# First norm's row factors moved behind the first matrix products of a fp32-split kernel, with nine low parts on GpSimd

## The reference, cut to what matters

```
xn = rmsnorm(x, norm1_g)                 # x * rsqrt(mean(x*x) + 1e-6) * g, per token
u  = xn @ w_in                           # 1024 x 5632
q_sb, k_sb, v_sb, f_raw, i_hg, q_hg, g_hg, gate_sb, gate_hg = split(u)
o_sb = stick_breaking_attention(q_sb, k_sb, v_sb)      # 8 heads of 64
o_hg = rmsnorm(hgrn2(silu(q_hg), 1-f, i_hg, log f)) * silu(g_hg)   # 4 heads of 128
h  = x + (sigmoid(gate_sb+b)*(o_sb @ w_o_sb) + sigmoid(gate_hg+b)*(o_hg @ w_o_hg)) @ w_out
```

## Time and profile before

| | |
|---|---|
| median of 3 runs | 1062.19 us (1062.15 to 1062.34) |
| the profiled execution's own time | 1062.51 us |
| its span in the trace | 1060.6 us |
| PE busy | 1049.5 us, 99% |
| DVE busy | 714.8 us, 67% |
| ACT busy | 596.8 us, 56% |
| POOL busy | 57.3 us, 5% |

### The profile page before, as it was taken

One profiled execution on the slowest core, in us unless ns is written; L12 is line 12 of the kernel. 1 busy time (PEld: TensorE's weight loads), 2 busy tenths in 40 slices (PEclk: granted clock), 3 DMA queues, 4 the chain that ended last, 5 costly groups with the idle time before them and its releaser, 6 DMA issues.

```text
span 1060.6 us, 16168 instructions
## 1 busy us (share of the span) xinstructions
PE 1049.5 (99%) x6582; PEld 926.2 (87%) x6582; DVE 714.8 (67%) x835; ACT 596.8 (56%) x754; POOL 57.3 (5%) x53
## 2 busy tenths in 40 slices
PE   9999999999999999999999999999999999999998
PEld 8897999888888889888888888899998888888888
DVE  6547786675656567966666666677888676666564
ACT  7558554454444356865754444476776564444464
POOL 0000001110000030002005000010000200000010
PEclk9999999999999999999999999999999999999999
DMA  8735444646564656345465565555424455555651
GB/s 270 257 120 184 134 159 126 213 137 220 173 221 161 200 162 207 127 128 201 159 198 200 186 210 190 168 173 185 160 81 154 134 185 198 173 199 174 211 171 41
DMA packets 131274, 184.32 MB, mean 174 GB/s; under 512 B 3200, under 2 KB 107904, under 8 KB 131200
## 3 DMA queue, kind: packets, MB, share of 16 engines
q1 hardware_dynamic: 130752, 182.68, 51.9%
q0 software_dynamic: 160, 0.52, 0.2%
q10 hardware_dynamic: 288, 0.07, 0.0%
HBM read 182.21 MB, written 1.05 MB: 173 GB/s over the span
## 4 chain that ended last, share of the span: by engine, by line
PE 90%; DVE 5%; ACT 3%; issue 2%; DMA 1%; SPq 0%; DVEq 0%; ACTq 0%
PE PS L375 88%; PE PS L383 2%; DVE WL L1730 1%; ACT WH L1129 1%; DMA RAW<-in_gla_w_in_dram 0%; DMA H<-in_x_dram 0%; DVE AR L1968 0%; DVE AR L2160 0%; ACT AR L1144 0%; DVE AR L2158 0%; DVE SC L2352 0%; ACT H L1439 0%; ACT X L1138 0%; DVE X L1742 0%; DVE AR L2152 0%
## 5 line engine op out<-in xcount | busy, mean ns | idle before, releaser
L1730 DVE TENSOR_TENSOR WL<-RAW,WH 128x2048 fp32r<-128x2048 f32 (+1 forms) x170 | 375.4, 2211 | 139.1 <-ACT WH L1129 138.6
L1129 ACT ACTIVATE WH<-RAW 128x2048 fp32r<-128x2048 f32 (+1 forms) x177 | 326.3, 1848 | 82.0 <-PE PS L375 77.6
L375 PE MATMUL PS<-WH,X 128*128 128x512 f32 (+1 forms) x1168 | 307.4, 346 | 0.6 <-issue 0.4
L375 PE MATMUL PS<-O,WH 128*128 128x512 f32 (+1 forms) x880 | 265.7, 363 | 0.2 <-DVE WL L1730 0.2
L375 PEld LDWEIGHTS PS<-WH,X 128*128 128x128 f32 x1168 | 204.6, 190 | 28.3 <-issue 2.1
L375 PE MATMUL PS<-X,WH 128*128 128x256 f32 (+1 forms) x864 | 218.2, 331 | 0.5 <-ACT X L1138 0.5
L375 PE MATMUL PS<-O,WL 128*128 128x256 f32 x744 | 203.3, 282 | 0.0
L375 PE MATMUL PS<-WL,X 128*128 128x512 f32 (+1 forms) x584 | 200.7, 344 | 0.0
L375 PEld LDWEIGHTS PS<-O,WH 128*128 128x128 f32 x880 | 156.1, 189 | 25.1 <-issue 0.7
L375 PE MATMUL PS<-X,WL 128*128 128x256 f32 x608 | 167.6, 282 | 0.0
L375 PEld LDWEIGHTS PS<-X,WH 128*128 128x128 f32 x864 | 145.1, 190 | 15.6 <-issue 0.9
(11 more groups left out here) (215 smaller groups left out, 764.0 us busy)
## 6 DMA issues: line engine op xcount, KB each, us to landing
RAW<-in_ffn_w_in_dram SPq DMA_DIRECT2D x44, 1024.0 KB, 5.1
RAW<-in_w_ff_dram SPq DMA_DIRECT2D x32, 1024.0 KB, 5.4
RAW<-in_ffn_w_out_dram SPq DMA_DIRECT2D x22, 1024.0 KB, 5.1
RAW<-in_w_in_dram SPq DMA_DIRECT2D x20, 1024.0 KB, 5.1
RAW<-in_gla_w_in_dram SPq DMA_DIRECT2D x12, 1024.0 KB, 5.3
RAW<-in_diff_w_in_dram SPq DMA_DIRECT2D x12, 1024.0 KB, 5.3
RAW<-in_ple_w_gate_dram SPq DMA_DIRECT2D x8, 1024.0 KB, 5.1
RAW<-in_w_out_dram SPq DMA_DIRECT2D x4, 1024.0 KB, 5.0
```

Source lines behind the costliest of these rows:

```text
L375: return e.matmul(o, l, r, start=start, stop=stop, skip_group_check=skip)
L1129: act(high, raw, ACT.Copy).then_inc(s["w_hi"], 1)
L1730: e.tensor_tensor(low, raw, high.bitcast(F32), ALU.subtract).then_inc(s["w_lo"], 1)
```

## The change

x is turned raw as it lands: first the blocks of x0, then of x1, and ACT and DVE split the turned blocks with the gain alone. DVE computes the row factors later (`first_norm`, after the low part of chunk 2), lays them out as RB by way of PE and ACT, and applies them where the products are read: a DVE `evac` multiplies the bank by RB for the 256-column forms (16 in all), ACT's `evac` of the long chunks (4, 5, 10 to 13) takes the factor as its scale. The gates' tanh stays on ACT, now in place in SBUF. The first chunk's first piece is loaded between x0 and x1, and the constants go ahead of chunk 4 where they went ahead of chunk 5. The low parts of chunks 6, 8, ... 22 of w_in move from DVE to POOL. Chunks 0 to 3 get banks 0, 1, 5, 6. The warm-up matmuls at the start are 8 and 3 where they were 24.

```diff
-POOL_LO = [AT["w_o_hg"] + 1, ...
+POOL_LO = [*(AT["w_in"] + n for n in range(6, 23, 2)), AT["w_o_hg"] + 1, ...
@@ tensor_program
-    for _ in range(WARM):                      # WARM = 24
-        mm(PS[:, 3, 0:128], m.ar(0, 128), m.ar(0, 128), True, True)
+    warm(WARM[0])                              # WARM = 8, 3
     e.wait_ge(s["d_idn"], 16)
+    e.wait_ge(s["d_x0"], 16)
+    turn_x(0, range(7))
+    warm(WARM[1])
+    e.wait_ge(s["d_x1"], 16)
+    first_chunk()
...
-    for n in range(4):
+    for n in range(1, 4):
         win(n)
+    e.wait_ge(s["d_con"], 16)
+    spread_r("n1", 2)
     first(4)
-    e.wait_ge(s["win_ev"], 4)
+    e.wait_ge(*evacuated(3))
     scores(0)
@@ scalar_program
     hi(w0 + 2)
-    evac(0)
     hi(w0 + 3)
-    evac(1)
+    rstd_y("n1")
+    spread_copy(0, 2)
     hi(w0 + 4)
-    evac(2)
     hi(w0 + 5)
...
     hi(w0 + 6)
     softplus(0)
@@ vector_program
+    def evac(n):
+        j, i = n % 2, n - 14
+        e.wait_ge(s["rb"], 1)
+        e.wait_ge(s["gemm"], w0 + n + 1)
...
+        e.scalar_tensor_tensor(out=dst, in0=v3(PS[:, WIN_BANK[n], :], 2), scalar=0.125 if n < 2 else 1.0,
+                               in1=m.RB[:, :].unsqueeze(1).to_broadcast([128, 2, 256]), op0=ALU.mult,
+                               op1=ALU.mult).then_inc(s["win_c"], 1)
-    for n in range(2, 6):
-        lo(w0 + n)
+    lo(w0 + 2)
+    first_norm()
+    lo(w0 + 3)
+    spread_diag(0, rstd_r("n1"))
+    lo(w0 + 4)
+    for n in range(4):
+        evac(n)
+    lo(w0 + 5)
     bounds()
-    lo(w0 + 6)
     softplus(0)
     lo(w0 + 7)
-    lo(w0 + 8)
     masked(0)
     softplus(1)
+    evac(6)
@@ gpsimd_program
+    for c in range(AT["w_in"] + 6, AT["w_in"] + 23, 2):
+        lo(c)
@@ sync_program
+    e.dma_start(H[:, 0, :], x_rows[:, 0, :]).then_inc(s["d_x0"], 16)
+    piece(0, 0)
+    e.dma_start(H[:, 1, :], x_rows[:, 1, :]).then_inc(s["d_x1"], 16)
```

More of the change, by code:

```diff
@@ L543, in spread_r, with turn_x, warm, first_chunk @@
         e.wait_ge(s["rb_d"], i + 1)
[L544 removed]
+        mm(PS[:, bank, 0:256], m.con("none"), m.ar(13888 if i < 2 else 8192, 256), True, True).then_inc(s["rb_m"], 1)
+    def turn_x(tb, ks):
+        for k in ks:
+            i = tr(turn_src(m, "n1", k)[:, 128 * tb:128 * tb + 128], m.tok(m.H)[:, tb, 128 * k:128 * k + 128])
+            if tb == 1:
+                i.then_inc(s["tr"], 1)
+    def warm(n):
+        for _ in range(n):
+            mm(PS[:, 0, 0:128], m.ar(0, 128), m.ar(0, 128), True, True)
+    def first_chunk():
+        (wh, wl), (high, low) = m.weights(0), m.pair("X")
+        for k in range(8):
+            turn_x(1, ((0, 1, 2, 3), (4, 5), (6,))[k] if k < 3 else ())
+            if k == 3:
+                turn_x(0, (7,))
+                turn_x(1, (7,))
+            if k % 2 == 0:
+                e.wait_ge(s[hi_done(0, k // 2)[0]], hi_done(0, k // 2)[1])
+            e.wait_ge(s["tr_hi"], k + 1)
+            for fb in range(2):
+                mm(PS[:, 0, fb * 256:fb * 256 + 256], wh[:, k, fb * 128:fb * 128 + 128], high[:, k, :], k == 0 and fb == 0, False, True)
+            if k % 2 == 0:
+                e.wait_ge(s[lo_done(0, k // 2)[0]], lo_done(0, k // 2)[1])
+            for fb in range(2):
+                mm(PS[:, 0, fb * 256:fb * 256 + 256], wl[:, k, fb * 128:fb * 128 + 128], high[:, k, :], False, False, True)
+            e.wait_ge(s["tr_lo"], k + 1)
+            for fb in range(2):
+                i = mm(PS[:, 0, fb * 256:fb * 256 + 256], wh[:, k, fb * 128:fb * 128 + 128], low[:, k, :], False, k == 7, True)
+        i.then_inc(s["gemm"], 1)
     e.wait_ge(s["warm"], 1)
[L548 to L549 removed]
+    warm(WARM[0])
     e.wait_ge(s["d_idn"], 16)
+    e.wait_ge(s["d_x0"], 16)
[3 more added lines that the diff above has]
+    first_chunk()
     qT, kT, v = (m.ar(o, 1024) for o in (0, 1024, 2048))
@@ L1825, in vector_program @@
     e.memset(m.ar(0, 128), 0.0).then_inc(s["warm"], 1)
[L1826 to L1839, removed]
-    e.wait_ge(s["d_g1"], 16)
[L1841 to L1855, removed]
+    lo(0, 0)
+    e.wait_ge(s["d_g1"], 16)
+    for j in range(4):
+        if j:
+            lo(0, j)
+        turn_lo("n1", 2 * j, 2 * j + 1)
+    for j in range(4):
+        lo(1, j)
     kh, qh, lf, bb, vh, GS, fr, ng = (m.ar(6528 + 1024 * i, 1024) for i in range(8))
@@ L2022, in vector_program @@
     factors(4)
+    evac(17)
     level(2)
     spans(6)
-    lo(w0 + 20)
     level(3)
+    evac(18)
     factors(5)
@@ L2031, in vector_program @@
     level(4)
-    lo(w0 + 22)
+    evac(19)
+    evac(20)
     level(5)
@@ L2036, in vector_program @@
     lo(w0 + 23)
+    evac(21)
     lo(w0 + 24)
@@ L2574, in sync_program @@
             e.wait_ge(s[lo_done(c - NR)[0]], lo_done(c - NR)[1])
-        n = PIECES.get(c, 1)
-        for j in range(n):
-            k1, kn = k0 + j * nk // n, nk // n
-            src = io[name][k1 * 128:(k1 + kn) * 128, n0:n0 + nn].rearrange("(k p) n -> p k n", p=128)
-            e.dma_start(m.chunk(c, j)[0].rearrange("p (k n) -> p k n", k=kn), src).then_inc(s[landed(c, j)[0]], 16)
+        for j in range(1 if c == 0 else 0, PIECES.get(c, 1)):
+            piece(c, j)
     o_rows = m.out.rearrange("(b p) d -> p b d", p=128)
```

190 lines of the change are left out of this document (90 added, 100 removed).

## The result

| | before | after |
|---|---|---|
| median | 1062.17 us (1062.15 to 1062.34) | 1072.47 us (1072.43 to 1072.83) |
| span of the profiled execution | 1060.6 us | 1070.7 us |

What follows compares the result with a forecast made beforehand. PE, busy for 99% of the span, was taken to bound the kernel. -3.6 + 0.4 + 4.9 + 4.1 = +5.8 us on 1062.51 gave 1068.3, 1068.0 as a median; range 1061.5 to 1073.0.

Steps and rivals of the forecast that it cites:

- Part A: At the start: sums of squares, factors and slicewise scaling leave the path, so PE's chunks begin earlier; -3.6 us.
- Part B: The matmul of `spread_r`, behind chunk 3, lies on PE's path; +0.4 us.
- Part C: Before chunk 4: its high part waits on ACT behind the copy of RB, so PE stands still; +4.9 us.
- forecast: The main case, all terms summed: 1068.0 us, own range 1065.5 to 1071, chance 0.48.
- second rival: The pause before chunk 4 lets PE fall to the slow pace, 1.7 us more: 1069.7 us; chance 0.18.
- Part D: Behind chunk 4: POOL's low parts and DVE's two-SBUF-input operations exclude each other, PE waits; +4.1 us, bounds 0 and 8.
- the added `evac` goes on beside POOL: DVE's added evacuation, 0.68 us with PSUM as one input, is not held off by POOL's low parts.
- the five places named: PE's waits: `sums(0)` 0.7, `sums(1)` 0.4, `values(3)` 0.3, `h_diag` to `level(2)` 1.4, `level(7)` 1.3 us.
- The first rival: The overlap of POOL and DVE costs nearly nothing: +1.7 to +2.4, 1063.3 to 1064.6 us; chance 0.20.
- The rule quoted in the prediction: A DVE instruction with two SBUF inputs and a GpSimd one reading SBUF contend for a port; the later blocks fully.
- The opposite reading: A tensor_tensor without a two-port mode is free, so the overlap term is about +0.7 us, one `evac` before `level(2)`.
- Costed at nothing: 1.2 MB (3.5 us) of constants ahead of chunk 4's load, SP waiting for POOL, and later stages: no cost.

Runs made afterwards that it cites:

- experiment 1: Changed kernel with the high part of chunk 4 ahead of the copy of RB on ACT: 1066.29 us.
- experiment 2: Changed kernel with the nine low parts of chunks 6 to 22 back on DVE: 1069.12 us.
- experiment 5: Changed kernel with chunk 4's high part ahead of the copy of RB and the nine low parts back on DVE: 1062.53 us.
- experiment 6: Changed kernel with unread matmuls of constants in PE's two long waits, 21 before chunk 4 and 8 ahead of `level(4)`: 1070.72 us.
- the reordering: Changed kernel with chunk 4's high part first, low parts on DVE, `spread_r` between chunks 2 and 3, less urgent work behind urgent: 1058.72 us.
- the table's difference column: Low parts on POOL against on DVE, in four pairs of kernels: 1.5, 3.8, 3.3 and 2.4 us more on POOL.

## Why the prediction was right, and where it was not

**Part A, the start.** Forecast -3.6, measured -3.4 (32.45 against 35.82, with no wait between), and -3.0 to -3.8 over the profiles of experiments 1, 2, 5 and 6. Two errors nearly cancel, which is luck. The transposes of x1 waited 0.19 us for their data until 7.70 instead of 6.8, so the first product began 0.95 us late, at 8.75 instead of 7.8; but it then ran at full pace at once, where I had let the slow one last to 9.2:

```profile
7.70 0.66 PE L394 MATMUL PS<-CON,H 128*128 128x128 f32 x4
8.13 0.84 ACT L1185 ACTIVATE X<-PS,SML 128x256 fp32r<-128x256 f32 x2 [1.33 <-PE PS L394]
8.75 0.47 PE L386 MATMUL PS<-X,WH 128*128 128x256 f32 x2 [0.39 <-ACT X L1185]
```

**Part B, `spread_r`.** 0.4 forecast; its row shows 0.59, like the earlier trace rows, and chunk 4 in the first experiment begins 0.24 behind it.

**Part C, the pause.** Right in place, cause and size: chain 5.3 forecast, 5.36 measured (32.45 to 37.81), idle 4.9 against 4.76. The first experiment shows the cause.

**The step that failed as a case: forecast and second rival were both true.** I gave the clock's fall 0.18 beside the forecast's 0.48, as if one excluded the other, and priced it once with 1.7 us. It happened, cost 1.5 us, and happened again behind `level(4)` for 1.4. The sixth experiment shows that they belong to PE's standing still. These 2.9 us, none of which was in the sum, are over half of the 4.5 by which the difference was missed (10.3 against 5.8). Part D's waits give 0.8, Part A 0.2 and Part C with B 0.1; 0.3 lies behind the ledger's last row and is not explained, and 0.2 is that the profiled execution before lay above its median. That the time still fell inside the range is owed to the range's top, which was set for the clock's fall with a dear Part D. The price itself was fair for this execution and too low in general: experiment 2's fall cost 2.8. And the sentence that the trace before has no pause above 1.1 us was a wrong reading: PE waits 1.36 us at 810.77 us there, and PEclk reads 1.00 from 808 to 816 us.

**Part D, the term that was mis-sized, and its cause half wrong.** 4.1 us forecast; in the ledger the waits and hand-overs behind chunk 4, without the clock, are 9.8 - 2.0 - 2.9 = 4.9. Experiment 6, with the pause as forecast and the clock up, gives 5.9 from chunk 4 to the turning (145.05 against 139.19), less the 0.5 of the long fillers: 5.4. With the pause gone too, experiment 1 gives 6.9 (146.12). I laid nearly all of it on POOL. Measured apart, without the pause, it is 3.6 for the evacuations alone (experiment 5) and 3.3 for POOL on top (3.8 by the medians). The sentence that failed is "the added `evac` goes on beside POOL", priced only where it stood ahead of `level(2)`: an evacuation isn't stretched by POOL, but it costs its 0.68 us in DVE's queue each time that PE waits for what is queued behind. Of the five places named, `sums(1)` 0.4 (forecast 0.4) and `values(3)` 0.4 (0.3) were right; `sums(0)` 0.7 was too much: the changed kernel has no wait there, the same pause with the clock up has 0.2 (experiment 6), and only without the pause it is 0.8 (experiment 1); `level(2)` to `level(4)` took 1.8 instead of 1.4 and `level(7)` 0.7 instead of 1.3. The turning, 0.8, was missed, and so were the hand-overs. It is on ACT's path: the last tanh now waits for DVE's evacuation, and `hi(w0 + 24)` behind it. Moving that ahead, with the rest of the reordering, removed it.

The first rival (no cost of the overlap) is refuted by the table's difference column, and its argument, that DVE is idle a third of the time, by where the idle third lies: in experiment 1 DVE is busy for 16.1 of the 18 us from 128 to 146 us. The rule quoted in the prediction (the Trainium skill, SBUF — State Buffer, section Who interferes with whom) holds here: the mask copy (L1919) takes 4.63 us beside a POOL operation of 4.61 and 0.74 alone, the mask product (L1913), a TENSOR_TENSOR with two SBUF inputs, 1.86 beside POOL and 0.69 alone. The opposite reading, +0.7, is refuted.

**Costed at nothing.** Right: the list of waits has no DMA for PE from 34 to 190 us, and the distances behind the hg branch are unchanged within 0.3 us.

## What to carry to other kernels

Moving a scaling behind a product puts the scale's broadcast in a queue: look at what stands behind that copy on the engine that makes it, and put whatever the bounding engine needs next in front. Work moved to an engine that is a third idle costs by its place in the queue and not by its share; count what PE awaits behind each inserted piece, and expect that a wait removed in one queue may come up in another. Cases of a forecast that can be true together should be summed, and a pause of the bounding engine be priced with the slow stretch behind it (1.5 and 2.8 us behind the same pause here).

## What the runs showed of the hardware that was not expected

- The clock's fall does not follow from the length of a wait alone, and the slow stretch behind a fall is not always as long: 1.5 us were lost behind the pause of 4.76 us in the changed kernel, 2.8 us behind the same pause in experiment 2. The wait ahead of `level(4)` is 2.02 us in the changed kernel and in experiment 1. Behind it the one reads 0.50, the other 1.00 (windows of PE, changed kernel and then experiment 1):

```profile
147.00:149.00 2.00, 2.00 (x10) 0.50 0.00 0
```

```profile
140.00:142.00 2.00, 1.95 (x39) 1.00 0.00 0
```

  What decides between them stays open. It may differ from one execution of the same kernel to the next: the mean granted clock of experiment 1's five executions is 1.000 in three (1066.02 to 1066.29 us) and 0.998 in two (1066.44 and 1066.56), but only the first was profiled.
- A COPY_PREDICATED with its mask and its data in SBUF is held off until POOL's operation ends (4629 ns against 741; it began 0.6 us after POOL's and ended 0.6 us after it), and so is a fp32 TENSOR_SCALAR with one SBUF tile and one factor per partition; the first of four took 2524 ns, beside POOL's 85.62 to 90.26, where the others took 342:

```profile
L1933 DVE TENSOR_SCALAR AR<-AR,SC x4: 340/342/2524, 87.9 to 90.9; 128x256 f32<-128x256 f32 x4
```

  An operation with PSUM as one input isn't: L1909 took 0.96 us at 47.34 beside POOL's 45.01 to 49.65, and 0.94 us at 58.78 with POOL idle.
